# Three moves in the hand-written order of a hybrid RWKV-7, Mamba-2 and short-convolution kernel

## The reference

```python
h = rmsnorm(x, norm_w[l])
p = h @ w_in[l]
oa = rwkv7_branch(...)        # a delta-rule recurrence, 16 heads of 64
ob = mamba2_branch(...)       # conv, gated state space, group norm
oc = short_conv_branch(...)   # bg * conv(cg * xin) * silu(g)
yb = einsum('btnw,nwd->btnd', stack([oa, ob, oc]), w_branch[l])
merged = sum(sigmoid(pg) * yb, over the branches)
x = x + merged @ w_out[l]
return rmsnorm(x, final_norm_w)
```

## Time and profile before

| | us |
|---|---|
| median of three runs | 1128.09 |
| the three runs | 1129.64, 1128.09, 1128.05 |
| the profiled execution, its time | 1129.64 |
| the profiled execution, its span | 1127.9 |
| TensorE busy | 1112.7 |
| VectorE busy | 809.9 |
| ScalarE busy | 606.6 |

### The profile page before, as it was taken

The page is one execution under the profiler, slowest core; times in us unless marked ns, Lnnn a source line. Parts: engine busy times, 40 slices in busy tenths (PEclk is TensorE's granted clock), DMA queues, the critical chain, the costliest instruction groups (busy, mean ns, idle before and its releaser), DMA issues.

```text
span 1127.9 us, 22732 instructions
## 1 busy us (share of the span) xinstructions
PE 1112.7 (99%) x7918; PEld 924.7 (82%) x7918; DVE 809.9 (72%) x1241; ACT 606.6 (54%) x915; POOL 42.2 (4%) x71
## 2 busy tenths in 40 slices
PE   7999999999999999999999999999999999999996
PEld 5888888888888888888888888888888888888885
DVE  4788889798898988979888846545555555556563
ACT  5666575665746657566564645444444444435443
POOL 3000000000100000000000020000000000000000
PEclk9999999999999999999999999999999999999998
DMA  7766556565465654656555564666666576657663
GB/s 197 201 162 183 151 153 161 151 168 163 130 171 160 169 159 134 173 158 168 144 159 157 154 197 154 210 189 202 188 193 185 179 221 189 192 181 284 200 192 107
DMA packets 254412, 197.24 MB, mean 175 GB/s; under 512 B 23095, under 2 KB 206624, under 8 KB 253856
## 3 DMA queue, kind: packets, MB, share of 16 engines
q1 hardware_dynamic: 251604, 195.81, 59.7%
q10 hardware_dynamic: 2764, 0.85, 0.4%
HBM read 193.71 MB, written 2.11 MB: 174 GB/s over the span
## 4 chain that ended last, share of the span: by engine, by line
PE 95%; DVE 2%; DMA 1%; issue 1%; ACT 1%; SPq 0%; ACTq 0%; DVEq 0%
PE ps L1344 29%; PE ps L1347 14%; PE ps L1438 12%; PE ps L1440 12%; PE ps L1439 12%; PE ps L1717 3%; PE ps L1715 3%; PE ps L1716 3%; PE ps L1471 1%; PE ps L1644 1%; PE ps L1327 1%; DMA o<-in_x 0%; PE ps L1500 0%; PE ps L1543 0%; PE ps L1370 0%
## 5 line engine op out<-in xcount | busy, mean ns | idle before, releaser
L837 DVE TENSOR_TENSOR wlo<-raw,whi 128x1024 fp32r<-128x1024 f32 (+1 forms) x356 | 436.3, 1236 | 224.0 <-ACT whi L450 222.1
L450 ACT ACTIVATE whi<-raw 128x1024 fp32r<-128x1024 f32 (+1 forms) x356 | 370.3, 1050 | 288.0 <-PE ps L1440 182.7
L1344 PE MATMUL ps<-hx,whi 128*128 128x512 f32 (+1 forms) x1440 | 522.3, 405 | 0.1
L1347 PE MATMUL ps<-hx,wlo 128*128 128x256 f32 (+1 forms) x1440 | 403.9, 280 | 0.0
L1344 PEld LDWEIGHTS ps<-hx,whi 128*128 128x128 f32 (+1 forms) x1440 | 268.9, 187 | 71.6 <-issue 8.3
L1347 PEld LDWEIGHTS ps<-hx,wlo 128*128 128x128 f32 (+1 forms) x1440 | 270.3, 188 | 2.4 <-DVE lots L1082 2.0
L1438 PE MATMUL ps<-whi,hx 128*128 128x512 f32 x384 | 150.9, 393 | 0.0
L1440 PE MATMUL ps<-whi,hx 128*128 128x512 f32 x384 | 149.5, 389 | 0.0
L1439 PE MATMUL ps<-wlo,hx 128*128 128x512 f32 x384 | 149.4, 389 | 0.0
L1440 PEld LDWEIGHTS ps<-whi,hx 128*128 128x128 f32 x384 | 72.1, 188 | 15.2
L1439 PEld LDWEIGHTS ps<-wlo,hx 128*128 128x128 f32 x384 | 72.1, 188 | 14.9
(11 more groups left out here) (282 smaller groups left out, 1054.4 us busy)
## 6 DMA issues: line engine op xcount, KB each, us to landing
raw<-in_w_in SPq DMA_DIRECT2D x548, 256.0 KB, 3.1
raw<-in_w_branch SPq DMA_DIRECT2D x96, 256.0 KB, 3.6
raw<-in_w_out SPq DMA_DIRECT2D x64, 256.0 KB, 3.6
o<-in_x SPq DMA_DIRECT2D x3, 1024.0 KB, 6.2
acb<-acs_rows SPq DMA_DIRECT2D x7, 256.0 KB, 3.4
out_y<-lots SPq DMA_DIRECT2D x5, 256.0 KB, 2.7
o<-in_x SPq DMA_DIRECT2D x2, 512.0 KB, 5.5
lots<-in_final_norm_w SPq DMA_DIRECT2D x1, 1024.0 KB, 10.3
```

The lines of the kernel that those rows point to most:

```text
L450: sc.activation(whi[:, slot, :, 0:width], raw[:, slot, :, 0:width], ACT.Copy).then_inc(hi_done, 1)
L837: tt(wlo[:, slot, :, 0:width], raw[:, slot, :, 0:width], whi[:, slot, :, 0:width].bitcast(F32), ALU.subtract).then_inc(lo_done, 1)
L1344: mm(ps[0:rows, bank, :], whi[:, slot, k, wcol], hx[:, kt].rearrange("p a t -> p (a t)"), start=first, stop=False, skip_group_check=True)
L1347: return mm(ps[0:rows, bank, 0:T], wlo[:, slot, k, wcol], hhi[:, kt, :], start=False, stop=last, skip_group_check=True)
```

## The change

Three things move in the written order, and nothing is added or taken away.

- ScalarE makes the scaled copy of g at t = 2, behind that of v, and not at t = 9. VectorE folds g at t = 1, behind v, and not at t = 5.
- VectorE folds tiles `nt` and `nt + 1` at t = 12, behind the last step of the solve and its copy, and not at t = 8, ahead of the solve.
- ScalarE's Tanh of tile `nt + 1`, which waits for that tile's fold, stands at t = 14 and not at t = 17.

```diff
--- before.py
+++ after.py
@@ -609,7 +609,6 @@
                             low_shift(1, half, BANKS[4], strip0 - 1)
                     if t == 2:
                         kept(j, 2)
-                    if t == 9:
                         kept(j, 3)
                     if t == 26:
                         act.wait_ge(s["bon_ok"], j + 1)
@@ -633,7 +632,7 @@
                     if t == 8:
                         low(strip0, 0, BANKS[0], xp[:, 3:3 + T])
                         low(strip0, 1, BANKS[0], zp[:, 0, :])
-                    if t == 17:
+                    if t == 14:
                         act.wait_ge(tile_out, nt + 2)
                         sc.activation(zp[:, 1, :], zp[:, 0, :], ACT.Tanh, scale=0.5).then_inc(s["halved"], 1)
                     if t == 10:
@@ -1057,7 +1056,6 @@
                         stt(bd, bv, -1.0, gg, ALU.mult, ALU.mult).then_inc(s["prod_ok"], 1)
                     if t == 1:
                         fold_shift(j, 2, BANKS[4])
-                    if t == 5:
                         fold_shift(j, 3, BANKS[4] + 1)
                     if t == 3:
                         shift(j, 2)
@@ -1125,8 +1123,6 @@
                         else:
                             gate_split(0, 0, y // 2 - nchunks + AHEAD)
                     if t == 8:
-                        fold(nt, BANKS[0], xp[:, 3:3 + T])
-                        fold(nt + 1, BANKS[0] + 1, zp[:, 0, :])
                         stt(bon, sh[:, 0, :], col(RK), k2, ALU.mult, ALU.mult).then_inc(s["rk_ok"], 1)
                     if t == 20:
                         fold(nt + 2, BANKS[1], scb[:, 0, :])
@@ -1144,6 +1140,8 @@
                         solve_corner(9)
                         dve.wait_ge(s["sol_r"], j * 9 + 9)
                         v.tensor_copy(sol_l, sol_t.rearrange("p s t -> p t s")).then_inc(s["sol_tr"], 1)
+                        fold(nt, BANKS[0], xp[:, 3:3 + T])
+                        fold(nt + 1, BANKS[0] + 1, zp[:, 0, :])
                     if t == 21:
                         dve.wait_ge(s["dat_ok"], 1)
                         dve.wait_ge(s["seg_e"], j + 1)
```

## The result

The changed kernel takes 1136.2 us in the median (1135.4 to 1137.2), the kernel before 1128.5 us in the same session. The ratio is 1.0067 (95% interval 1.0050 to 1.0085), which is 7.6 us (the two medians are 7.8 us apart). Forecast were 6.2 us more, 1134.3 us, and a range of 1130.6 to 1137.2 us.

The account below looks back on a forecast made before the run. TensorE, busy 1112.7 of 1127.9 us, waits at L1082 for a slackless chain through the solve. Terms 0.03 + 0.69 + 0.06 = 0.78 us, eight times, add 6.2 to 1128.09: 1134.3 us, range 1130.6 to 1137.2.

Parts of the forecast that it names:

- The chain: Solve, copy, ScalarE's DMA issues, split c10, L1072, conv, split, L1082, TensorE: no slack, so added time counts eight times.
- c10: ScalarE's split queued behind its DMA issues of L662, with VectorE's half following; a link between copy and L1082.
- The two folds bring nothing: Ahead of the solve: taking away their 0.67 us leaves VectorE waiting for L293's matrix; 0.10 us allowed for earlier landing.
- Rival A: At the solve's start: it does start earlier, 0.59 us; 0.16 us an iteration, kernel 1.3 us slower; chance 0.15.
- From the copy to the issues: ScalarE's Tanh waits for both folds ahead of L662's issues: 0.69 us later, plus 0.06 us for the Tanh's dispatch.
- rival B: At L662: the issues wait for the Tanh to end, 1.13 us an iteration, 9.0 us in all; chance 0.09.
- Rival C: SyncE's and ScalarE's DMA issues, now 0.7 us apart, become cheaper: 0.59 us comes back an iteration; chance 0.03.
- The start of the solve: At L1011: g's move delays L293's second pair 0.08 to 0.20 us; with the landing allowance, +0.03 us an iteration.
- TensorE's wait at step 5: At the first scores, 0.42 us later: TensorE might stand 0.1 us, time it would later spend at L1082 anyway.
- TensorE's wait at step 16: For the first fold before writing bank 0: 0.4 to 0.5 us, part of L1082's lateness, not an addition.
- Sum: Main loop: 0.03 + 0.69 + 0.06 = 0.78 us an iteration, eight iterations, 6.2 us slower.
- The main case: Whole kernel: 0.78 us an iteration, own range 0.5 to 0.95 us, 1132.1 to 1135.7 us; chance 0.73.

Follow-up runs that it names:

- e7: The kernel before with ScalarE's split c10 moved ahead of its wait for the copy and the DMA issues: 0.9981, 2.1 us faster.
- e6: The changed kernel with SyncE's load of the second quarter issued behind both pairs of L293, not between them: 1.0004 to the kernel before.
- e11: The changed kernel with split c10 early and SyncE's second-quarter load behind both pairs of L293: 0.9990 to the kernel before.
- e12: The kernel before with both folds and g moved, the Tanh left at t = 17, SyncE's second-quarter load behind both L293 pairs: 0.9988.
- e4: The changed kernel with its Tanh back at t = 17: 1.0030 to the kernel before, 3.4 us slower.
- e1: The kernel before with only the two folds moved behind the copy: 1.0009, 1.0 us slower.
- e8: The changed kernel with split c10 ahead of ScalarE's wait for the copy: 1.0036 to the kernel before, 4.1 us slower.
- e3: The kernel before with only the Tanh moved to t = 14: 1.0002, no difference.
- e10: The kernel before with split c10 early and SyncE's second-quarter load behind both pairs of L293: 0.9976, 2.7 us faster.

## Why the prediction was right

*The chain.* Right. L1080 is 6.77 us behind ScalarE's issues as before, and whatever was added ahead of them came out at the end. e7 shows the other side: take out its link c10 and the kernel is 2.1 us faster, where TensorE had waited 2.0 us for L1082. The prediction took the chain to bind in the eighth iteration too, without a row for it. It does: in that iteration the kernel before has a wait of 0.75 us at L1554 instead, and there is another of 0.78 us in the first (the row `PEld ps L1554 <- issue` above). The prediction's sentence that the other matmuls follow each other without a gap passes over both.

*The two folds bring nothing.* Right, and the step that decided the sign. The prediction took the landing from the one row where VectorE had waited for it, 1.87 us behind the issue, and not from the fastest small DMA. With the folds gone VectorE waits at that place in all eight iterations, and the landing takes 1.61 to 2.18 us, about 1.86 in the middle. Rival A, that the solve starts earlier, is out for this kernel (idle time stands ahead of the first L1010 of each iteration), but e6 shows how near it was: with another order of SyncE it comes true, and the kernel is at +0.5 us, where A had +1.3. From the start of the last issue, an estimated half of 1.32 us behind 394.91, the landing took 398.15 - 395.57 = 2.6 us here, and in e6, with the load behind the pair, at most 1.46 us and some 0.65 us of issue, about 2.1. The Trainium skill ("DMA: Bandwidth & Descriptors", "Anatomy of one DMA — SWDGE (gpsimd) path") gives a fixed cost of about 2.0 us, but for a DMA that GpSimd issues; SyncE issues these, so it is no figure for them, and it could not have told the 2.6 us from the 2.1.

*From the copy to the issues.* Forecast 0.69 + 0.06 us, measured 1.08 - 0.42 = 0.66 us. The Tanh holds the issues back by 0.01 us; rival B is out by the two rows at 408.31 and 408.32. Rival C is out as well: the pair lasts 1.27 us though SyncE issues its own 0.68 us earlier.

*The start of the solve.* This is the term that was mis-sized: 0.03 us forecast; measured from the L1080 before, the solve starts 0.06 to 0.36 us later in the second to seventh iteration, 0.25 in the mean. Of the term's two parts it is the issue that was off. The second pair goes 0.28 us later (394.91 - 344.88 against 391.91 - 342.16), not 0.13: the first pair is 0.40 us later, 0.42 forecast, but SyncE then starts the load 0.27 us behind the end of that pair (393.57 to 393.84), where I had allowed at most 0.17, and the second pair follows the load's end by 0.11 us in both kernels. And the landing gives back 0.04 us in the mean, where I had allowed 0.10. The second scores do not hold the pair: their reduction ends at 394.51, before the load's issue does. TensorE's wait at step 5, which I had put at 0 to 0.1 us, is 0.19 us; that it is made up for later holds in this kernel, but not in e11 and e12.

*TensorE's wait at step 16.* Forecast 0.4 to 0.5 us, seen 0.72 us (0.41 to 0.72 in the second to seventh iteration, 1.1 in the first and last), as it inherits the late start of the solve. It is not an addition in the changed kernel (e4 has the same wait and 4.2 us less time), as said. It would be one without the Tanh's wait: e1's 1.0 us and most of e8's 4.1.

*Sum.* Forecast 0.78 us an iteration, eight times, 6.2 us. Measured in the profiles: 0.25 + 0.66 = 0.91 us in the mean of the first six periods; 0.57 us in the last, where the kernel before already waited for the landing; and 1.17 us in the first iteration, from ScalarE's L565 ahead of the loop to the first L1080. L565 starts at 93.88 us in the kernel before and here at

```profile
92.68 0.34 ACTq L565 DMA_DIRECT2D acs_rows<-acs  x1
```

That is 7.2 us of the 7.6. (The two profiled executions are only 5.9 us apart because the one of the kernel before reached the loop 1.2 us later. e3, as fast as the kernel before, has 92.87 there, and over all runs the place lies between 92.4 and 95.3.) So the iterations do not cost the same, as the prediction had them.

*The range.* The main case had its own range, up to 1135.7 us. The measured 1136.2 us lies above it, in the part that was added for rival B, which did not happen. Counted as a difference, 7.6 us is the main case's upper bound, 0.95 us an iteration. The mechanism was right; that the time fell inside the whole range owes something to a rival that is out.

## What to carry to other kernels

When work is taken from in front of a wait, look for one execution in which that wait was exposed, and read its length there; the work may have been covering a transfer, and then moving it gains nothing and whatever it now stands before pays. A cheap instruction with a wait in an in-order queue costs what is queued behind it: here a free Tanh put two DMA issues and a split behind two folds, and the three moves cost twice the sum of what they cost alone. And before reordering the slow engine, move what an idle engine could do earlier (c10): it cost nothing and was worth 2.1 us.

## What the runs showed of the hardware

- A pair of 8 KB DMAs issued behind 512 KB of loads on the same queue landed 1.61 to 2.18 us after its issue ended (changed kernel, eight iterations), with the loads behind it in 1.46 or 1.47 us at most in six of eight iterations (e6; 1.70 in the first, 1.24 in the last). In a timeline the issue looks the same (1.32 and 1.28 us for the pair).
- ScalarE's DMA issues run beside an activation that was dispatched just before them: Tanh at 408.31, issue at 408.32. The next activation waits for the issues: 409.72, 0.13 us behind their end.
- Kernels with a weight load 0.18 us late at step 5 have periods 0.13 to 0.14 us longer than e10 without it (e11, e12); removing the wait of the earlier trace rows, 0.28 us idle, took 0.23 us off the period (69.20 to 68.96, e7).
